# A two-block transformer kernel on one core: three PSUM banks for attention scores and two for turned weights, quadrant gates, a two-pass gate tile, later weight splits

## The reference

```python
def block_diag_linear(x, w, b):            # w: 8 blocks of 64 x 64
    xb = x.reshape(x.shape[:-1] + (LRU_BLOCKS, LRU_BLOCK))
    y = jnp.einsum("bsni,nij->bsnj", xb, w.astype(x.dtype))
    return y.reshape(x.shape) + b.astype(x.dtype)
...
    r = jax.nn.sigmoid(block_diag_linear(xf, w_a, b_a))
    i = jax.nn.sigmoid(block_diag_linear(xf, w_i, b_i))
...
    proj = x @ w_in                        # nsa_mixer: 1024 query columns, then 48 gate columns
    q = proj[..., :H * d].reshape(B, S, G, R, d)
    gate = jax.nn.sigmoid(proj[..., H * d:].astype(jnp.float32)).reshape(B, S, G, R, 3)
...
        p_c = masked_softmax(s, dist_c >= 0)          # compressed keys
        p_s = masked_softmax(s, mask_s)               # selected keys
        p_w = masked_softmax(s, mask_w)               # window
        o = gg[..., 0:1] * o_c + gg[..., 1:2] * o_s + gg[..., 2:3] * o_w
    return o @ w_out
```

## Time and profile before

| | us |
|---|---|
| median of 3 runs | 2038.97 |
| lowest and highest | 2037.82, 2039.61 |
| the profiled execution's own time | 2038.9 |
| its span, first to last instruction | 2037.1 |
| PE busy in it | 2018.7 (99%) |
| DVE busy, ACT busy | 1079.5 (53%), 829.4 (41%) |

### The profile page before, as it was taken

The page is one execution under the profiler, slowest core; times in us unless marked ns, Lnnn a source line. Parts: engine busy times, 40 slices in busy tenths (PEclk is TensorE's granted clock), DMA queues, the critical chain, the costliest instruction groups (busy, mean ns, idle before and its releaser), DMA issues.

```text
span 2037.1 us, 26626 instructions
## 1 busy us (share of the span) xinstructions
PE 2018.7 (99%) x10576; PEld 1697.4 (83%) x10576; DVE 1079.5 (53%) x1866; ACT 829.4 (41%) x1385; POOL 16.8 (1%) x31
## 2 busy tenths in 40 slices
PE   9999999999999999999999999999999999999998
PEld 7788888888888888889888888888788898888887
DVE  6665444443465465444744432387778666444323
ACT  5644333332334334334433322354777664333222
POOL 0000000000000000000000000000000000000000
PEclk9999999999999999999999999999999999999999
DMA  4223233323332222223233333353110023333232
GB/s 164 76 77 107 88 99 93 102 87 96 115 94 79 78 93 88 72 94 104 83 96 100 93 96 96 97 170 117 29 56 23 12 94 99 97 93 103 87 100 73
DMA packets 53546, 184.47 MB, mean 91 GB/s; under 512 B 6010, under 2 KB 8330, under 8 KB 53168
## 3 DMA queue, kind: packets, MB, share of 16 engines
q1 hardware_dynamic: 50976, 171.99, 27.4%
q0 software_dynamic: 2160, 10.63, 1.6%
q10 hardware_dynamic: 288, 0.17, 0.0%
HBM read 180.62 MB, written 2.14 MB: 90 GB/s over the span
## 4 chain that ended last, share of the span: by engine, by line
PE 93%; DVE 3%; issue 1%; ACT 1%; DVEq 0%; ACTq 0%
PE bank L518 70%; PE bank L538 6%; PE bank L687 6%; PE bank L1070 2%; PE bank L1052 1%; PE bank L927 1%; PE bank L1037 1%; PE bank L1038 1%; PE bank L915 1%; PE bank L963 1%; PE bank L1022 0%; DVE WL L1724 0%; DVE SS L2464 0%; PE bank L1023 0%; PE bank L1073 0%
## 5 line engine op out<-in xcount | busy, mean ns | idle before, releaser
L1724 DVE TENSOR_TENSOR WL<-RAW,WH 128x1024 fp32r<-128x1024 f32 (+1 forms) x320 | 384.0, 1204 | 459.1 <-ACT WH L1133 458.1
L518 PE MATMUL bank<-AH,WH 128*128 128x512 f32 x1456 | 568.5, 394 | 1.0 <-DVE XP L1779 1.0
L518 PE MATMUL bank<-AL,WH 128*128 128x512 f32 x1456 | 562.3, 390 | 0.0
L518 PE MATMUL bank<-AH,WL 128*128 128x512 f32 x1456 | 561.7, 390 | 0.0
L1133 ACT ACTIVATE WH<-RAW 128x1024 fp32r<-128x1024 f32 (+1 forms) x320 | 331.3, 1041 | 492.6 <-PE bank L518 418.4
L518 PEld LDWEIGHTS bank<-AH,WH 128*128 128x128 f32 x1456 | 273.3, 188 | 59.7 <-issue 4.0
L518 PEld LDWEIGHTS bank<-AH,WL 128*128 128x128 f32 x1456 | 273.4, 188 | 57.4
L518 PEld LDWEIGHTS bank<-AL,WH 128*128 128x128 f32 x1456 | 273.4, 188 | 55.2 <-issue 0.7
L1779 DVE TENSOR_TENSOR T<-bank,RS 128x512 f32<-128x512 f32 x156 | 106.3, 687 | 165.9 <-PE bank L518 165.9
L518 PE MATMUL bank<-HH,WH 128*128 128x512 f32 x484 | 188.3, 389 | 0.0
L518 PE MATMUL bank<-HLO,WH 128*128 128x512 f32 x484 | 188.3, 389 | 0.0
(11 more groups left out here) (400 smaller groups left out, 2835.2 us busy)
## 6 DMA issues: line engine op xcount, KB each, us to landing
RAW<-in_ffn_in SPq DMA_DIRECT2D x132, 512.0 KB, 3.6
RAW<-in_ffn_out SPq DMA_DIRECT2D x48, 512.0 KB, 3.5
RAW<-in_ret_t SPq DMA_DIRECT2D x32, 512.0 KB, 3.6
RAW<-in_ffn_out SPq DMA_DIRECT2D x24, 384.0 KB, 3.2
RAW<-in_ret_v SPq DMA_DIRECT2D x16, 512.0 KB, 3.7
RAW<-in_ret_out SPq DMA_DIRECT2D x16, 512.0 KB, 3.6
RAW<-in_w_in_t SPq DMA_DIRECT2D x13, 512.0 KB, 4.1
RAW<-in_nsa_t SPq DMA_DIRECT2D x9, 512.0 KB, 3.6
```

The costliest lines, as they stand in the source:

```text
L518: t = e.matmul(BANK[b][:, :], wt[:, sl], xx[:, slot(kk) if name == "nsa_out" else kk, :], start=kk == 0 and n == 0, stop=kk == kt - 1 and ...
L1724: e.tensor_tensor(WL[w][:, 0:n], RAW[r][:, 0:n], WH[w][:, 0:n], ALU.subtract).then_inc(w_low.did(v))
```

## The change

1. The scores' ring has three banks (0, 1, 2), the turned weights' ring two (3, 6).
2. The recurrence's gates are computed by four multiplies of a 64x64 block for each f in place of two of 128x128: row halves and column halves of the array are used apart, and the second gate's two halves come out swapped. ACT takes that gate in two instructions of 64 partitions, which swap them back; its bias is stored swapped. `bd` has half the columns and needs no zeroing.
3. The gate tile keeps its weights' remainder in WH itself, in the zero columns 64 to 111 of each slice, so two multiplies a slice do for three. DVE adds the two parts (a copy, a sum and the scaling in place of the scaling).
4. In the attention loop DVE's remainders of later query weights come two steps later.

```diff
+        LOW, UP = slice(0, 64), slice(64, 128)
-        TURN_BANKS = (2, 3, 6)
+        SCORE_BANKS, TURN_BANKS = (0, 1, 2), (3, 6)
...
-                e.matmul(BANK[b][:, :], bd[:, f, :], y[:, :], start=True, stop=True).then_inc(
+                enter(b + 1, ("lru_i", f))
+                e.matmul(BANK[b][LOW, :], bd[LOW, f, :], y[LOW, :], start=True, stop=True)
+                e.matmul(BANK[b][UP, :], bd[UP, f, :], y[UP, :], start=True, stop=True).then_inc(
                     matmul.did(("lru_a", f)))
-                enter(b + 1, ("lru_i", f))
-                e.matmul(BANK[b + 1][:, :], bd[:, 4 + f, :], y[:, :], start=True, stop=True).then_inc(
+                e.matmul(BANK[b + 1][UP, :], bd[LOW, 4 + f, :], y[LOW, :], start=True, stop=True)
+                e.matmul(BANK[b + 1][LOW, :], bd[UP, 4 + f, :], y[UP, :], start=True, stop=True).then_inc(
                     matmul.did(("lru_i", f)))
...
+            def gate_tile():
+                u, b = p.first["nsa_t", 8], p.bank["nsa_t", 8]
+                w = p.slot[u]
+                enter(b, ("nsa_t", 8))
+                e.wait_ge(*w_low.at(u))
+                for kk in range(8):
+                    sl = slice(kk * 128, (kk + 1) * 128)
+                    e.wait_ge(*x_high.at(("q", kk)))
+                    e.matmul(BANK[b][:, :], WH[w][:, sl], AH[:, kk, :], start=kk == 0, stop=False)
+                    e.wait_ge(*x_low.at(("q", kk)))
+                    t = e.matmul(BANK[b][:, :], WH[w][:, sl], AL[:, kk, :], start=False, stop=kk == 7)
+                t.then_inc(matmul.did(("unit", u), ("nsa_t", 8)))
...
-            tile("nsa_t", 8, A, split_of("q"))
+            gate_tile()
...
-                b = next_bank("score", (0, 1), ("small", f))
+                b = next_bank("score", SCORE_BANKS, ("small", f))
...
-                b = next_bank("score", (0, 1), ("att", s))
+                b = next_bank("score", SCORE_BANKS, ("att", s))
...
-                e.activation(g[:, :], BANK[b + 1][:, :], ACT.Sigmoid, bias=V("lru_bi", f)).then_inc(
-                    free_a.did(("lru_i", f)))
+                for own, other in ((LOW, UP), (UP, LOW)):
+                    e.activation(g[own, :], BANK[b + 1][other, :], ACT.Sigmoid,
+                                 bias=V("lru_bi_swapped", f)[other]).then_inc(free_a.did(("lru_i", f)))
...
+                    if v == p.first["nsa_t", 8]:
+                        wide, raw = (t.rearrange("p (k c) -> p k c", c=128) for t in (WH[w][:, :], RAW[r][:, :]))
+                        e.tensor_tensor(wide[:, :, 64:112], raw[:, :, 0:48], wide[:, :, 0:48], ALU.subtract).then_inc(
+                            w_low.did(v))
+                        continue
...
-            e.tensor_tensor(T[1][0:48, :], BANK[p.bank["nsa_t", 8]][0:48, :], RS[0:48, :], ALU.mult).then_inc(
-                free_v.did(("nsa_t", 8)))
+            e.tensor_copy(T[1][0:48, :], BANK[p.bank["nsa_t", 8]][64:112, :]).then_inc(kv_v.did("low gates"))
+            e.wait_ge(*kv_v.at("low gates"))
+            e.tensor_tensor(T[1][0:48, :], T[1][0:48, :], BANK[p.bank["nsa_t", 8]][0:48, :], ALU.add).then_inc(
+                kv_v.did("gates"))
+            e.wait_ge(*kv_v.at("gates"))
+            e.tensor_tensor(T[1][0:48, :], T[1][0:48, :], RS[0:48, :], ALU.mult).then_inc(free_v.did(("nsa_t", 8)))
...
-                if queries_before(s):
-                    before("nsa_t", queries_before(s))
-                if s == 6 * PAIR + 9:
+                if s > 1 and queries_before(s - 2):
+                    before("nsa_t", queries_before(s - 2))
+                if s == 6 * PAIR + 11:
                     before("nsa_out", 0)
```

More of the change, by code:

```diff
@@ L30 @@
     ("ffn_post0", 8), ("kv_norm", 8), ("mix_pre1", 8), ("mix_post1", 8), ("ffn_pre1", 8), ("ffn_post1", 8),
-    ("conv_w", 16), ("conv_b", 4), ("lru_ba", 4), ("lru_bi", 4), ("lru_lambda", 4), ("b_alpha", 2),
+    ("conv_w", 16), ("conv_b", 4), ("lru_ba", 4), ("lru_bi_swapped", 4), ("lru_lambda", 4), ("b_alpha", 2),
     ("gla_norm", 1), ("pe_k", 16), ("pe_v", 16), ("pe_k_swapped", 16), ("pe_v_swapped", 16),
@@ L233, in build @@
             SG = sb("SG", [128, 2, 8, 128], stack=ar)
-            bd = sb("bd", [128, 8, 128], stack=ar)
+            bd = sb("bd", [128, 8, 64], stack=ar)
             wal = sb("wal", [16, 256], stack=ar)
@@ L441, in pool_program @@
         def pool_program(e):
-            e.memset(bd[:, :, :], 0.0).then_inc(zeroed.did("bd"))
-            e.wait_ge(*zeroed.at("bd"))
             e.wait_ge(s_x[7], 16)
@@ L447, in pool_program @@
                     rows = slice(64 * half, 64 * half + 64)
-                    e.dma_start(bd[rows, 4 * i:4 * i + 4, rows],
+                    e.dma_start(bd[rows, 4 * i:4 * i + 4, :],
                                 D[name].rearrange("(f a) i j -> a i f j", a=2)[half]).then_inc(s_bd, 16)
@@ L2636, in laid_out @@
         "conv_w": a["conv_w"][0].reshape(4, 4, 128).transpose(2, 1, 0).reshape(128, 16),
-        "conv_b": cols(a["conv_b"][0]), "lru_ba": cols(a["lru_ba"][0]), "lru_bi": cols(a["lru_bi"][0]),
+        "conv_b": cols(a["conv_b"][0]), "lru_ba": cols(a["lru_ba"][0]), "lru_bi_swapped": cols(a["lru_bi"][0].reshape(8, 64)[np.arange(8) ^ 1].reshape(512)),
         "lru_lambda": cols(a["lru_lambda"][0]), "b_alpha": cols(a["gla_b_alpha"][0]),
```

## The result

| | median us | runs from .. to |
|---|---|---|
| before | 2039.29 (4 runs) | 2037.82 .. 2040.40 |
| changed | 2051.58 (4 runs) | 2047.47 .. 2053.00 |

The ratio is 1.0063, with an interval of 1.0051 to 1.0075: the changed kernel is 12.3 us slower by the medians. The prediction was 2040.9 with a range of 2034.8 to 2046.2, and the median lies 5.4 us above that range. In the prediction's terms this is "slower" (over 2043.0), to which it gave 0.32. The profiled execution took 2050.35 us with a span of 2048.6.

A forecast was written before the change was run, and what follows sets the result against it. PE, busy 99% of the span, was taken to bound the kernel. From 2038.9 us, gate tile -1.8, recurrence's gates -2.2, rings +6.0 and later remainders 0 gave 2040.9 us, range 2034.8 to 2046.2.

The forecast's parts named there:

- Gate tile, -1.8: Gate tile: PE loses 8 of 24 multiplies at 0.23 us each, DVE's longer work is covered; -1.8 us.
- Quadrant gates, -2.2: Recurrence's gates: four multiplies run at once on quadrants, 4.6 us in place of 6.8; -2.2 us.
- a microsecond taken from PE's list [...] moves the end by a microsecond: Whole kernel: with PE busy 99%, work removed from or waits added to PE's list shift the end one for one.
- Rings, +6.0: Attention: removed waits for scores' banks against added waits for turned banks, replayed on PE's order; sum +6.0 us.
- The turn of step 58: Attention, step 58: the turn waits for an earlier copy and moves 0.56 us later; net +0.21 after a removed scores' wait.
- the compressed turn: Attention, steps 65 and 66: compressed weights' turn waits for a copy, the turn after it starts 0.66 us later.
- a pair: Attention, each pair of heads: shorter turned ring costs +0.87 us net, counted six times as +5.2.
- The third bank removes that: Attention, steps 17 and 18: scores' 0.75 us wait goes, but a later turn waits for its copy, +0.79.
- Nobody on PE waits for either after the third bank: 0: Attention, later remainders: 1.23 us of DVE work moved before step 60's scores delays nothing on PE; 0 us.
- ACT gets ahead: Attention rival: step 58's scores taken 3 us sooner let ACT run ahead, rings cost only +0.3; 2035.2 us, chance 0.18.
- The clock: Attention rival: added waits bring three more 3.41 us stretches at granted clock 0.50, +5.1; 2046.0 us, chance 0.24.
- the addition is small: Argument against the clock's rival: only 0.21 us of waiting is added behind compressed scores, in five pairs.

The follow-up runs named there:

- the filled kernels: Kernel before with two score and two turned banks (2047.51 us), plus unused multiplies in PE's waits: 2045.80 us with late waits filled, 2043.77 us with early ones too.
- rings alone: Kernel before with three banks for scores and two for turned weights, nothing else: 2047.74 us, ratio 1.0053.
- before with copies ahead: Kernel before with each turn's copy moved in front of the exponential before it on ACT's list: 2039.11 us, ratio 1.0002.

## Why the prediction was wrong

**Gate tile, -1.8: right** (-1.81).

**Quadrant gates, -2.2: mechanism right, size wrong**, -1.4. PE's work shrank by 2.3, near what was worked out, and going in and out of the quadrants cost 0.36 us each time (1.68 less two slots of 0.23 and 0.86 for the eight instructions; forecast 0.39). The sentence on draining that the prediction takes from the Trainium skill stands in TensorEngine Tiling under "Tiling Modes", Key Properties, not under "Overview". The step that failed is taking PE's saving as time saved: "a microsecond taken from PE's list [...] moves the end by a microsecond". Before the tile of tokens at 78.4 PE already waited 0.3 us for DVE, and DVE's list doesn't move, so 0.9 of the saving of f = 0 and 1 stays there.

**Rings, +6.0: right in sum** (+5.8 of waits), less so in the parts. The turn of step 58 is 0.56 later as replayed, the compressed turn waits 0.5 to 0.6; a pair costs 0.67 in place of 0.87. "The third bank removes that" was a credit for nothing, since two banks do the same.

**"Nobody on PE waits for either after the third bank: 0": wrong**, and the first of the two large errors. I followed the moved 1.23 us to PE's scores only, whose bank is indeed free. But ACT's exponential also waits for DVE, and behind it on ACT's list stands a copy that frees a turned bank. The step that failed is this nothing: by the runs the moved remainder costs 3.1 to 3.6 us alone and 6.1 to 6.9 with the short ring, of which part is clock, and with the copies ahead of the exponentials about 0.5. The rival "ACT gets ahead" had the sign wrong for the same reason: ACT gets later.

**The clock: the second error**, priced as a rival (0.24, +5.1 for three more pieces) and not in the sum. Against it I held that "the addition is small". In fact PE now waits 0.77 and 1.46 us at steps 17 and 18 (0.75 and 0.91 before), and the filled kernels show that such waits lower the clock over the runs, though not in each. In the profiled run five pieces in place of three are 4 to 5 us.

Together, for the profiled runs' +11.4: tile and gates -3.25, rings +5.8, remainders +2.5, their working on each other about +1.2 (0.14 to 0.21 us a pair beyond the two alone), and the clock from what is left, 5.2. Read directly it is 4.3: the two pairs that hold the pieces take 28.47 and 29.35 us, 6.9 more than rings and remainders would give, and the three pieces of before cost 2.6. All but the first of these rest on differences of single traces and are good to a microsecond or so.

## What to carry to other kernels

A ring's banks are freed by an instruction on another engine's in-order list, so look at what stands ahead of that instruction and what it waits for; before a ring is made shorter, move the freeing copies to the head of their step. When work is moved on an engine, follow every consumer of what it delays, and then what is queued behind each of these on its own engine. And price PE's waits twice: once as waits, and once as what they may do to the granted clock.

## What was not expected of the hardware

- Multiplies without a use, put into PE's waits of 0.4 to 1.5 us, made the kernel faster: 2047.5 to 2043.8 us, mean granted clock from 0.994-0.996 to 0.997-0.998.
- One and the same kernel (rings alone) ran from 2042.7 to 2052.3 us on one chip, with mean granted clocks from 0.998 to 0.992: about 1.6 us for each 0.001. (One reading does not fit such a line: a run of before with copies ahead has 0.970 at 2039.8 us, as long as its neighbours.) With few runs of such a kernel the median says little, and its waits are better read from a trace together with its count of half-clock pieces.
- Four 64x64 float32 multiplies on different quadrants start within 0.02 us of each other, also where they write to two banks.
